# Opening stage of a three-block transformer kernel: input in two channel halves behind one norm vector, products in turn with transposes, angles after the input

## The reference, cut to what matters

```python
meta = jnp.broadcast_to(meta_tokens[None].astype(x.dtype), (B, N_META, D_MODEL))
h_res = jnp.concatenate([meta, x], axis=1)                  # 16 + 512 tokens, 1024 channels
pos = jnp.concatenate([meta_pos, positions + N_META], axis=1)
for l in range(DEPTH):
    h = rmsnorm(h_res, norm_gain[l])
    proj = h @ w_in[l]
    u_pool, z_pool, c_q, c_kv, k_rope, z_mla, g_pool, g_mla = jnp.split(proj, IN_SPLIT_POINTS, axis=-1)
    ...
    o_mla = mla(c_q, c_kv, k_rope, pos, ...)                # needs cos and sin of pos * inv_freq
```

## Time and profile before

| | |
|---|---|
| runs, median (lowest to highest) | 1836.28 us (1833.15 to 1836.44), 3 runs |
| the profiled execution | its time is known by its span, 1830.6 us, 5.7 below the median of the runs |
| TensorE busy | 1762.0 us (96%) |
| TensorE weight loads | 1504.5 us (82%) |
| VectorE, ScalarE, GpSimd busy | 1187.4 (65%), 875.0 (48%), 331.4 us (18%) |
| chain that ended last | PE 51%, DVE 5%, ACT 4%, issue 1%, DMA 1% |
| DMA | 241.46 MB, mean 132 GB/s |

### The profile page before, as it was taken

How to read it: one execution, slowest core, us unless ns; L and a number is a source line. 1 busy time by engine, 2 the same in 40 slices (tenths; PEclk the granted TensorE clock), 3 DMA queues, 4 the chain that set the end, 5 groups by cost and what they waited for, 6 DMA issues and landing times.

```text
span 1830.6 us, 27554 instructions
## 1 busy us (share of the span) xinstructions
PE 1762.0 (96%) x11270; PEld 1504.5 (82%) x11270; DVE 1187.4 (65%) x1704; ACT 875.0 (48%) x1407; POOL 331.4 (18%) x223
## 2 busy tenths in 40 slices
PE   8999999999999999999999999999999989999993
PEld 6998788999998888999999776765568867888882
DVE  5566645554366655544676598586764457888896
ACT  5425444234334444334343365556553246878771
POOL 3333222002243222001000276310010000000001
PEclk9999999999999999999999999999999989999997
DMA  6203112223312202323222210213142359999994
GB/s 188 76 24 99 47 47 79 84 70 116 96 59 75 70 25 69 100 93 98 93 83 80 69 47 24 67 48 99 63 172 93 115 195 346 403 402 404 403 384 173
DMA packets 156104, 241.46 MB, mean 132 GB/s; under 512 B 9593, under 2 KB 101018, under 8 KB 155978
## 3 DMA queue, kind: packets, MB, share of 16 engines
q1 hardware_dynamic: 148602, 212.88, 33.9%
q0 software_dynamic: 4464, 16.25, 2.3%
q10 hardware_dynamic: 2912, 10.55, 1.4%
HBM read 223.41 MB, written 16.25 MB: 131 GB/s over the span
## 4 chain that ended last, share of the span: by engine, by line
PE 51%; DVE 5%; ACT 4%; issue 1%; DMA 1%; POOL 0%; POOLq 0%; ACTq 0%; DVEq 0%
PE acc L1358 15%; PE acc L856 10%; PE acc L1101 9%; PE acc L1126 7%; PE acc L1190 2%; PE acc L1204 2%; PE acc L1221 1%; PE acc L1344 1%; PE acc L1212 1%; PE acc L1086 1%; DVE upad L2681 1%; DVE qk L2681 0%; ACT v L1954 0%; PE acc L1008 0%; DVE qk L2679 0%
## 5 line engine op out<-in xcount | busy, mean ns | idle before, releaser
L856 PE MATMUL acc<-h_split,ring_split 128*128 128x264 f32 x1088 | 308.2, 283 | 0.0
L856 PEld LDWEIGHTS acc<-h_split,ring_split 128*128 128x128 f32 x1088 | 204.3, 188 | 0.0
L856 PE MATMUL acc<-h_split,qk_split 128*128 128x264 f32 x384 | 109.5, 285 | 1.3 <-DVE ring_split L2188 1.3
L856 PE MATMUL acc<-ring_split,qk_split 128*128 128x264 f32 x384 | 108.8, 283 | 0.0
L1126 PE MATMUL acc<-ring_split,h_split 128*128 128x256 f32 x384 | 107.9, 281 | 0.0
L856 PE MATMUL acc<-h_split,krope_split 128*128 128x264 f32 x320 | 93.4, 292 | 1.7 <-POOL ring_split L3010 1.6
L856 PE MATMUL acc<-ring_split,krope_split 128*128 128x264 f32 x320 | 90.7, 284 | 0.0
L2188 DVE TENSOR_TENSOR ring_split<-ring,o_split 128x1024 fp32r<-128x1024 f32 (+1 forms) x32 | 44.8, 1417 | 65.3 <-ACT o_split L1520 65.1
L3120 POOL DMA_INDIRECT latent<-h_rows,rows_of x16 | 18.1, 1129 | 355.8 <-PE acc L1344 214.1
L2188 DVE TENSOR_TENSOR ring_split<-ring,qk_split 128x1024 fp32r<-128x1024 f32 (+1 forms) x56 | 59.4, 1070 | 34.1 <-ACT qk_split L1520 34.1
L2996 POOL TENSOR_TENSOR latent<-latent 128x528 f32<-128x528 f32 x18 | 26.8, 1490 | 300.1 <-ACT latent L1515 299.8
(11 more groups left out here) (597 smaller groups left out, 5741.4 us busy)
## 6 DMA issues: line engine op xcount, KB each, us to landing
ring<-in_w_in SPq DMA_DIRECT2D x64, 1024.0 KB, 5.2
ring<-in_w_expert_gate SPq DMA_DIRECT2D x10, 2048.0 KB, 13.7
ring<-in_w_expert_up SPq DMA_DIRECT2D x10, 2048.0 KB, 13.9
ring<-in_w_expert_down SPq DMA_DIRECT2D x10, 2048.0 KB, 14.7
ring<-in_w_out SPq DMA_DIRECT2D x12, 1024.0 KB, 5.0
y_rows<-gate ACTq DMA_DIRECT2D x16, 512.0 KB, 6.8
hres<-in_w_expert_up SPq DMA_DIRECT2D x3, 2048.0 KB, 12.9
qk<-in_w_expert_down SPq DMA_DIRECT2D x3, 2048.0 KB, 14.5
```

Source lines behind the costliest of these rows:

```text
L856: ins = nc.tensor.matmul(dst[0:rows_, half, 0:HALF], w[:, k, :], x[:, c], start=(k == 0 and i == 0), stop=(k == last and i == 2), skip_gro ...
```

## The change

It moves the following. SP issues a small gain vector and the identity first, then cq0 and cq1, then positions and the rest of const, cq2 and cq3, and only then waits for vrows and loads the other gains. ScalarE's queue loads meta, then x in two halves of 512 channels, each with its own semaphore. The first norm gain has a transpose of its own ("first_gain"), and "vecs" goes into turn_tables. ScalarE splits the first weights ahead of h. TensorE turns only chunks 0 to 3 of x before the products, with fillers between, and each later one inside first_products, ahead of the product of k = 0 to 3, in an accumulator that an earlier x chunk had. The angles are kept in v and worked out by VectorE behind the last h_lower; their sines come on ScalarE behind chunk 4 of the latents. In layer 0 the sum of squares is used behind chunk 4 instead of chunk 2. The layer's vectors (lv, small) are copied behind the tables.

```diff
--- before.py
+++ after.py
@@ -274,6 +274,8 @@
...
         vrows2 = qkf[:, 5 * D + P:5 * D + 2 * P]
+        first_gain = qkf[:, 5 * D + 2 * P:5 * D + 3 * P]
+        angles = v[:, :, :].rearrange("p c t -> p (c t)")[NOPE:QK, 0:2 * T].rearrange("p (a t) -> p a t", a=2)
@@ -306,6 +308,7 @@
...
         X_BY_ACT = (2, 5, 7)
+        SUMS_AT = (4, 2)
...
@@ -391,7 +394,10 @@
...
         const_loaded = sem("const_loaded")
-        x_loaded = sem("x_loaded")
+        x_loaded = [sem(f"x_loaded{i}") for i in range(2)]
+        meta_loaded = sem("meta_loaded")
+        ident_loaded = sem("ident_loaded")
+        first_gain_loaded = sem("first_gain_loaded")
         vec_loaded = sem("vec_loaded")
...
@@ -631,17 +637,17 @@
...
         def _(sp):
-            sp.dma_start(const[:, :], a["const"][:, 0:K_TIE]).then_inc(const_loaded, 16)
-
-            sp.dma_start(krope[NOPE:QK, 0, META:T].bitcast(I32),
-                         a["positions"].to_broadcast([ROPE, SEQ])).then_inc(const_loaded, 16)
-
-            sp.wait_ge(pool_made, at(pool_made, "vrows"))
-            for l in range(LAYERS):
+            sp.dma_start(first_gain[0:DC, :], a["norm_gain"][0].rearrange("(k m) -> k m", k=DC))\
+                .then_inc(first_gain_loaded, 16)
+            sp.dma_start(const[:, 0:P], a["const"][:, 0:P]).then_inc(ident_loaded, 16)
+
+            def load_gains(l):
                 r = LV * l
...
                                        ("q_norm_gain", 20, 1, QK), ("k_norm_gain", 21, 1, QK)):
+                    if (l, name) == (0, "norm_gain"):
+                        continue
                     sp.dma_start(vrows[r + r0:r + r0 + k, 0:m],
...
@@ -667,6 +673,13 @@
...
             load_first(0, 2)
+            sp.dma_start(angles[:, 0, META:T].bitcast(I32),
+                         a["positions"].to_broadcast([ROPE, SEQ])).then_inc(const_loaded, 16)
+            sp.dma_start(const[:, P:], a["const"][:, P:K_TIE]).then_inc(const_loaded, 16)
+            load_first(2, 4)
+            sp.wait_ge(pool_made, at(pool_made, "vrows"))
+            for l in range(LAYERS):
+                load_gains(l)
             for name, r0, k in (("norm1_gain_2", V_N1, DC), ("norm2_gain_2", V_N2, DC), ("b_gates_2", V_BG, 16),
...
@@ -677,7 +690,6 @@
...
             mark(vec_loaded, "vec2", 0)
-            load_first(2, 4)
             for i, name in enumerate(("lambda_q1_2", "lambda_k1_2", "lambda_q2_2", "lambda_k2_2")):
...
@@ -806,6 +818,15 @@
...
+            def accumulator_again(label, reader, back):
+
+                for x in jobs[-back]:
+                    released(*x)
+                slot = (len(jobs) - back) % ACCS
+                jobs[-back] = [(label, reader, n.layer)]
+                n.slots[label, n.layer] = slot
+                return acc[:, slot, :, :]
+
...
@@ -862,6 +883,10 @@
...
                 for k in range(DC):
+                    if n.layer == 0 and k < 4:
+                        here, n.layer = n.layer, None
+                        turn_input(k + 4)
+                        n.layer = here
                     pe.wait_ge(dve_made, at(dve_made, ("hlow", k)))
...
@@ -883,25 +908,43 @@
...
             pe.wait_ge(dve_made, at(dve_made, "blank"))
-            dst = accumulator("vecs", dve_evacuated)
-            keep_busy(dst[:, 1, :], 7, work[:, 0, 0:512])
-            pe.wait_ge(const_loaded, 32)
-            pe.wait_ge(gains_loaded, at(gains_loaded, "gains"))
-            done(nc.tensor.transpose(dst[:, 0, 0:LAYERS * LV], vrows[0:LAYERS * LV, :],
-                                     ident[0:LAYERS * LV, 0:LAYERS * LV]), "vecs")
-            pe.wait_ge(x_loaded, 80)
+            dst = accumulator("first_gain", dve_evacuated)
+            keep_busy(dst[:, 1, :], 5, work[:, 0, 0:512])
+            pe.wait_ge(ident_loaded, 16)
+            pe.wait_ge(first_gain_loaded, 16)
+            done(nc.tensor.transpose(dst[:, 0, 0:DC], first_gain[0:DC, :], ident[0:DC, 0:DC]), "first_gain")
             dst = accumulator("meta", dve_evacuated)
+            pe.wait_ge(meta_loaded, 16)
             for c in range(DC):
...
             done(ins, "meta")
-            for c in range(DC):
-                dst = accumulator(("x", c), act_evacuated if c in X_BY_ACT else dve_evacuated)
+
+            def turn_input(c):
+
+                if c % 4 == 0:
+                    pe.wait_ge(x_loaded[c // 4], 16)
+                by = act_evacuated if c in X_BY_ACT else dve_evacuated
+                if c < 4:
+                    dst = accumulator(("x", c), by)
+                else:
+                    dst = accumulator_again(("x", c), by, 4 - c % 2)
                 for i in range(4):
...
+
+            for c in range(4):
+                turn_input(c)
+                keep_busy(acc[:, 3, 1, 0:256], 1 if c < 2 else 0, work[:, 0, 0:256])
+            keep_busy(acc[:, 3, 1, :], 3, work[:, 0, 0:512])
+
...
+                pe.wait_ge(const_loaded, 32)
+                pe.wait_ge(gains_loaded, at(gains_loaded, "gains"))
+                dst = accumulator("vecs", dve_evacuated)
+                done(nc.tensor.transpose(dst[:, 0, 0:LAYERS * LV], vrows[0:LAYERS * LV, :],
+                                         ident[0:LAYERS * LV, 0:LAYERS * LV]), "vecs")
                 pe.wait_ge(vec_loaded, at(vec_loaded, "vec2"))
...
@@ -924,7 +967,7 @@
...
                     product_split(("c", c), act_evacuated, h_up, h_low)
-                    if c == 2:
+                    if c == SUMS_AT[n.layer]:
                         product("ss_h", act_evacuated, [ones[:, :]], lambda k: sum_sq,
...
@@ -1497,16 +1540,19 @@
...
-            for i in range(4):
-                act.dma_start(xin[:, i, :], a["x"][0, i * P:(i + 1) * P, :]).then_inc(x_loaded, 16)
-            act.dma_start(metain[0:META, :], a["meta_tokens"]).then_inc(x_loaded, 16)
-            act.wait_ge(dve_made, at(dve_made, "angles"))
-
-            nc.scalar.activation(sinT, krope[NOPE:QK, 0, :], ACT.Sin).then_inc(act_made, 1)
-            mark(act_made)
-            nc.scalar.activation(cosT, krope[NOPE:QK, 1, :], ACT.Sin, scale=-1.0,
-                                 bias=small[NOPE:QK, 0:1]).then_inc(act_made, 1)
-            mark(act_made, "trig")
+            act.dma_start(metain[0:META, :], a["meta_tokens"]).then_inc(meta_loaded, 16)
+            for i in range(2):
+                act.dma_start(xin[:, :, i * HID:(i + 1) * HID],
+                              a["x"][0, :, i * HID:(i + 1) * HID].rearrange("(j p) d -> p j d", p=P)).then_inc(x_loaded[i], 16)
+
+            def rotation_tables():
+
+                act.wait_ge(dve_made, at(dve_made, "angles"))
+                nc.scalar.activation(sinT, angles[:, 0, :], ACT.Sin).then_inc(act_made, 1)
+                mark(act_made)
+                nc.scalar.activation(cosT, angles[:, 1, :], ACT.Sin, scale=-1.0,
+                                     bias=small[NOPE:QK, 0:1]).then_inc(act_made, 1)
+                mark(act_made, "trig")
...
@@ -1567,7 +1613,10 @@
...
-            act.wait_ge(dve_evacuated, at(dve_evacuated, "vecs"))
+            n.layer = 0
+            weights_upper(JOBS_A, 0)
+            n.layer = None
+            act.wait_ge(dve_evacuated, at(dve_evacuated, "first_gain"))
             act.wait_ge(dve_evacuated, at(dve_evacuated, "meta"))
...
@@ -1581,8 +1630,8 @@
...
                 h_upper(c, None)
-                if c in (0, 1, 4):
-                    weights_upper(JOBS_A, (0, 1, 4).index(c))
+                if c in (0, 4):
+                    weights_upper(JOBS_A, (None, 0, 4).index(c))
                 n.layer = None
...
@@ -1607,7 +1656,11 @@
...
                     weights_upper(JOBS_A, c + 3)
-                    if c == 2:
+                    if c == SUMS_AT[n.layer]:
+                        if n.layer == 0:
+                            n.layer = None
+                            rotation_tables()
+                            n.layer = 0
                         root("ss_h", inv[:, :], D, 1)
...
@@ -2157,30 +2210,32 @@
...
-            dve.wait_ge(const_loaded, 32)
...
-            result("vecs")
-            slot = n.slot(("vecs"))
-            evacuated(nc.vector.tensor_copy(vecs[:, :], acc[:, slot, 0, 0:LAYERS * LV]), "vecs")
+            def rotation_angles():
+
+                dve.wait_ge(const_loaded, 32)
+                ang, turns = trig[NOPE:QK, 0, :], trig[NOPE:QK, 1, :]
+                nc.vector.tensor_copy(ang[:, 0:META], const[NOPE:QK, K_META:K_META + META])
+                chain(nc.vector.tensor_copy(ang[:, META:T], angles[:, 0, META:T].bitcast(I32)))
+                chain(ts(ang[:, META:T], ang[:, META:T], float(META), None, ALU.add))
+                chain(ts(ang, ang, const[NOPE:QK, K_FREQ:K_FREQ + 1], None, ALU.mult))
...
+                made(stt(out=angles[:, 1, :], in0=angles[:, 0, :], scalar=-1.0,
+                         in1=angles[:, 0, :], op0=ALU.mult, op1=ALU.max), "angles")
+
+            result("first_gain")
+            slot = n.slot(("first_gain"))
```

(23 more changed lines are left out.)

31 lines of the change are left out of this document (12 added, 19 removed).

## The result

The changed kernel takes 1838.64 us, median of 14 runs (1837.85 to 1839.67); the kernel before, run on the same chip beside it, 1833.81 us, median of 14 (1832.67 to 1837.21). The ratio is 1.0023, with a 95% interval of 1.0015 to 1.0031: slower, by 4 to 5 us. The profiled execution of the changed kernel took 1838.8 us with a span of 1837.0.

A forecast was written before the change was run, and what follows sets the result against it. TensorE bounds from 100 us on, so chunk 6's start in the opening decides: 67.5 against 60.7, taken as +6.5 us; span 1830.6 becomes 1837.1, plus 5.7 gives 1842.8 us. Own range 1840.5 to 1845; 8-in-10 range 1834.5 to 1846.5.

The forecast's parts named there:

- The likeliest case: Opening: squares don't move and late sines delay chunk 5; chunk 6 at 67.5 against 60.7; chance 0.47 with clock variants.
- C: Time at which the first weights, cq0, land in the opening: 12 us, with 9 as the lower bound.
- shared by bytes: Rival on the opening's loads: queues share by bytes, cq0 lands at 9 us; 1838.4 to 1841.0 us; chance 0.22.
- Start of products, sum: Opening: products start at about 17.5 instead of 22.27, squares at 25.7, GpSimd's sum is done at 38.0.
- the port: GpSimd's sum beside VectorE's angles: four adds lose 0.3 us each, 1.2 us in all.
- S: Start of the fourth product (chunk 3): 41.5 us instead of 43.32, when weights 3 are split behind the sum.
- Lock by the letter: Rival on GpSimd's sum: each of seven adds delayed by a whole VectorE angle operation, 3.5 us; 1845 us; chance 0.12.
- Behind chunk 4: Sines, table loads and root take 6.64 us before chunk 5, as a fourth accumulator waits; lower clock adds 1.75 us.
- Reaches the end unchanged: TensorE is busy 1671 of 1731 us from 100 us on, so a microsecond lost before reaches the end unchanged.
- from span to runs: Final step: profiled span 1830.6 becomes 1837.1; the runs' median stood 5.7 above the span, giving 1842.8 us.
- +6.5 us: Total loss taken at chunk 6's start, between +6.8 us and, at full clock, +6.2.
- The other side: Rival: TensorE bounds the whole opening, so the products' 6.8 us earlier end goes through; 1829.5 us; chance 0.12.

The follow-up runs named there:

- before_late_sines: The kernel before with sine and cosine on ScalarE behind chunk 2's result instead of at the start; 1839.76 us, ratio 1.004.
- sines_c2: The changed kernel with sine and cosine behind chunk 2's result instead of chunk 4's; 1835.85 us, ratio 1.0008.
- vecs_c3: The changed kernel with the gains' transpose behind chunk 3, so three accumulators instead of four are taken behind chunk 4; 1837.68 us, ratio 1.0019.
- tuned_squares: The changed kernel with angles behind weights 5, sines and gains' transpose behind chunk 3, weights 6 before the reciprocal, four squares in ScalarE's pauses; 1827.1 us, ratio 0.9964.
- h_first: The changed kernel with four upper halves of h and their squares before ScalarE's first weights, VectorE's weights 0 and 1 behind h_lower 2; 1843.57 us, ratio 1.0049.
- combined: The changed kernel with h_first, sines_c2 and vecs_c3 together and VectorE's weights 6 ahead of the reciprocal; 1837.63 us, ratio 1.0017.
- fillers_c3: The changed kernel with five filler matmuls in TensorE's idle stretch ahead of chunk 3; 1836.54 us, ratio 1.0015.
- delay9: The kernel before with ten filler matmuls (8.6 us together) ahead of chunk 5 in layer 0; 1840.1 us, ratio 1.0043.
- slot_shift: The kernel before with the turn of the four accumulators begun one place further on; 1831.25 us, ratio 0.9984.

## Why the prediction came out as it did

**Direction and main chain: right.** The likeliest case was slower, by an opening whose squares don't move and whose sines stand behind chunk 4. This is what the trace shows; before_late_sines, sines_c2 and vecs_c3 show the part of the sines and the fourth accumulator by itself, and tuned_squares that of the squares.

**Loads: right.** C was 12, measured 12.56. From 8 to 10 us the two queues of the changed kernel moved

```profile
q10 hardware_dynamic: 256, 0.52, 67.2%
q1 hardware_dynamic: 261, 0.27, 37.8%
```

256 packets of 2 KB beside 261 of 1 KB: as many of one as of the other, and the rival "shared by bytes" falls. This bears on the page of the Trainium skill that I had weighed ("DMA: Bandwidth & Descriptors", section "Queues, rings and completion order"). The going round between queues agrees with these counts; that four rows of 1 KB go for one of 2 KB does not. Whether an engine takes one row of each queue at a turn or the same number of several, the counts don't tell.

**Start of products, sum: right within 1 us.** Products at 16.8 and 18.1 for 17.5; squares 25.45 for 25.7; sum 37.54 for 38.0, of which the port 1.0 for 1.2; S = 41.09 for 41.5. That the port's term came out so near is in part luck, since it was priced as four adds of 0.3 and was seven adds that lost 0.05 to 0.35 us each. "Lock by the letter" had the right kind of event and named only one of the engines that it can hold: VectorE's angle operations went from 0.43 to 1.46, the three of L2230 from 2.17 to 5.18, and its whole row of angles took 12.9 us where the prediction counted on 5.9. It ended 0.36 us before it would have held weights 3; in h_first and combined it did hold them. I had taken only one half of the rule of the Trainium skill ("SBUF — State Buffer", section "SBUF: two separate sides"): whichever starts first, a GpSimd operation or a VectorE one that is two-port or has two inputs, has the shared port pair for its whole length, and the other is blocked. The trace agrees: the add that began at 26.77 ended at 28.16, and VectorE's operation that began at 26.98 ended only at 28.44.

**A clock term that was missing: 2.1 us.** The prediction let TensorE idle from about 38 to 41.5 and then had the fourth product at full clock. It charged the clock for the later gap and not for this one. From start to result chunk 3 took 8.24 us instead of 6.11; fillers_c3 brings it back to 6.1. On the other hand it expected 3.9 us of lower clock at the first products, and there was none: TensorE idled 2.71 us in front of them, and from 18.34 on the matmuls are 0.12 us apart. So the third product was through 1.5 us earlier than forecast and the idle stretch was 4.60 us long.

**Behind chunk 4: right to 0.1 us in the wait, short by 0.4 in the clock.** From chunk 4's result (55.13) to the root's end it was 6.64 us, exactly the sum from the earlier trace rows. Chunk 5 took 8.13 us from start to result, 2.1 us more than before (55.03 to 61.03), for which I had 1.75. VectorE's steps behind the root did not bind, as said. So at chunk 5's result the loss was 8.9 us for 6.8 forecast: 2.1 + 0.4 less 0.4 for S.

**"Reaches the end unchanged": a step that failed, by 2.4 us** (and 0.5 more at 583). delay9 shows that most of a delay alone does reach the end (6.9 of 8.5 us from 583 on); slot_shift shows what broke the rule: the change also turns the accumulators, and with them the order of two engines at 1040. The span came out as 1837.0 for 1837.1 by luck, because these 2.9 us and the missing clock terms nearly cancel.

**The step that failed and put the time off: from span to runs.** 1842.8 was forecast and 1838.64 measured, 4.2 us less. The prediction set the span of one execution, 1830.6, against the median of other runs, 1836.28, and carried their difference, 5.7 us, as if it lay around every span. Around the span lie 1.8 to 2.0 us (1838.8 against 1837.0, 1836.67 against 1834.7). The rest was that the median of three runs was high and the profiled execution among the short ones of this kernel: 1830.6 + 1.8 = 1832.4. On that base the same +6.5 us gives 1838.9. Put in medians: the 14 runs of the kernel before have 1833.81, 2.5 us below the 1836.28 that the forecast started from, and the change cost 4.8 us and not 6.5, since the profiled execution of before was 1.4 shorter than its median. The range, which spans all this, held.

**The other side: refuted here, its condition nearly right.** I had asked for squares by 19.5 to 20.5 us and for sines before the end of chunk 4. In tuned_squares the first square is at 16.3 (the last four from 25.7), the sum is there at 32.24, and the fourth product follows the third without a wait at 35.97. The sines, from 48.15 to 49.41, are still behind chunk 4's last matmul (47.84) and cost the 0.8 us of idle time shown there. Up to chunk 4 TensorE bounds the opening, as that case says. What the change left out is not the earlier products but the four squares that had pauses to go into, together with moving the angles and sines off the chain.

**What remains open.** How the turn of the accumulators shifts the two engines by the 0.17 us that decide at 1040, and why the clock's low stretch in the router stage lasts 10 us in one execution and 17 in the next.

## What to carry to other kernels

To bring an engine's first work forward helps only as far as the chain that frees its output comes forward too: follow the work that is late next, and ask for each step put off (here sines with a table load) which wait it becomes. Price every idle stretch of TensorE of a few us with its clock as well, by a row of the same kernel where the clock fell, or put fillers in it. When a row of small operations is moved beside another engine's work, measure its length there, and not where it ran alone: the angles took 12.9 us for 5.9. Take the overhead around a span from one execution's time and span, never from a median of others.

## What the hardware showed that I had not expected

- Two engines at SBUF: whichever of VectorE's two-input operation and GpSimd's began first, by 0.04 to 0.13 us, decided whether VectorE took 2.88 or 0.75 us, and it did so in the same way in every trace of a kind. A change of bookkeeping was worth 2.4 us there, half of the 4.8 us that the change under study cost.
- Beside a row of GpSimd adds of 1.4 us, a chain of small VectorE operations lost about 1.0 us per operation (0.43 to 1.46), and GpSimd 0.05 to 0.35 per add.
- An idle stretch of 4.6 us left 23 matmuls in the next 5 us, at 1.2 GHz; ten matmuls of 512 columns (the five fillers) in its place kept 2.4 GHz throughout. An idle stretch of 2.7 us ahead of the first products of the same kernel left the clock as it was.
